# Four of six token-scale rows by two DMAs through DRAM in place of a product with ones, and the gate chain of the forgetting attention one step later

## The chip, the cores and the metric

One core of one Trainium2 chip runs the whole program. The metric is the device time of one execution in microseconds (us); lower is better. TensorE (PE) multiplies, VectorE (DVE) and ScalarE (ACT) work element by element, GpSimd (POOL) does small odd work, and SyncE (SP) issues nearly all DMAs. On a text's engine names, PE, DVE, ACT, POOL and SP are these five.

## What is computed

A trunk of two layers over 512 tokens of 1024 features. Each layer adds half a gated feed-forward network (FFN), a mixer (forgetting attention in the first layer, a sliding-window attention in the second), and half another FFN; a norm stands ahead of each of the six steps and one at the end. Cut to what matters here:

```python
def rms_norm(x, g):
    y = x * lax.rsqrt(jnp.mean(x * x, axis=-1, keepdims=True) + RMS_EPS)
    return y * g

for i in range(2):
    h = h + 0.5 * swiglu(rms_norm(h, norm_g[i, 0]), ffn_w_in[i, 0], ffn_w_out[i, 0])
    h = h + mixer_i(rms_norm(h, norm_g[i, 1]))
    h = h + 0.5 * swiglu(rms_norm(h, norm_g[i, 2]), ffn_w_in[i, 1], ffn_w_out[i, 1])
return rms_norm(h, final_g)

# in the forgetting attention, ahead of the scores:
log_f = log_sigmoid(f_logit + b_f)      # f_logit: 16 of the projected columns
c = cumsum(log_f, axis=time)
```

## The kernel before, in words

**Layout.** The residual `h` lies transposed in SBUF: 128 partitions are features, the free dimension is the 512 tokens, in 8 blocks. A norm is split in two: the gain goes into the activations ahead of the products (`u_hi`, `u_lo`), and the scale of each token, 1/sqrt(mean square), is applied to the result of the products. Every value in a product is split into a high and a low part, so one 128x128 by 128x512 step is three matmuls (`products`, L498).

**Units.** The weights come in 355 units of mostly 128x1024 floats. SP loads a unit into one of four slots of `raw` (L328), ACT rounds it into one of two slots of `w_hi` (L1114), DVE subtracts to get `w_lo` (L1546), PE uses it (24 matmuls for a unit of the FFN input) and counts `unit_used`. ACT takes unit n+2 when unit n has been used. SP may load unit n+4 when `w_lo` of unit n is there (`w_ready`). Each engine's program is written out by hand, so the order of the text is the order on the engine, and semaphores tie them together.

**An FFN** (`ffn`, `in_body`) runs 11 bodies of four units: two units make the gate products in banks 0 and 1, two the up products in banks 2 and 3. DVE multiplies the gate banks with `rstd_row` (L1650), ACT takes silu, DVE multiplies the up banks (L1655) and so on. PE may write the gate banks again, in the next body, when both gate products are scaled (`gate_scaled`). The first body is peeled off, because the token scales are made within it.

**The token scales.** `rstd_row` is the row of 512 scales on all 128 partitions. It is made six times, once for each norm ahead of an FFN or a mixer, numbered nn = 0 to 5:

1. PE sums the squares of each token (`token_sums`, L518) into bank 5, after unit 1 of an FFN body, or after the gate unit of the forgetting attention.
2. DVE makes the mean square `ms` (L1578), POOL raises it to the power -0.5 (`pow_rstd`, L453): `rstd`, 128 partitions by 4, tokens on partitions.
3. DVE scales the identity with each of the four columns (`diagonals`, L1585): `diag`, 128x512.
4. PE multiplies `diag` with a matrix of ones (`row_sums`, L524), so that each partition gets the whole row, in bank 5. In an FFN this stands after unit 2 of the first body.
5. ACT copies it to `rstd_row` (`row_copy`, L1180).

**The forgetting attention** (`fox`) projects V in eight units (k = 0 to 7), with the gate unit (16 columns) after k = 0 and the first query and key units after k = 4. While PE does this, DVE and ACT run the gate chain on 16 partitions: scale and bias, the parts of log-sigmoid (L1765 to L1771 on DVE, Exp and Ln at L1320 and L1323 on ACT), the cumulative sum (L1811 to L1815) and its split (L1327, L1818). V of k = 0 to 3 is scaled out of banks 0 to 3 after k = 3 (ACT L1332, DVE L1825: `v_ready`), and the query unit after k = 4 needs bank 0 of these free.

The lines quoted here say where PE stands in the FFN:

```python
                        mm.then_inc(unit_used, 1)
                        if peeled and r == 1:
                            token_sums(nn, 5)
                        if peeled and r == 2:
                            row_sums(nn)
```

## Time and profile before

| | |
|---|---|
| median of 3 runs | 1869.68 us (1867.63 to 1871.52) |
| the profiled execution | 1868.03 us |
| its span, first to last instruction | 1866.2 us |
| granted TensorE clock over the span | 0.999 |
| PE busy | 1849.2 us, 99% |
| DVE, ACT busy | 926.1 us (50%), 696.1 us (37%) |
| DMA | 181.85 MB, mean 97 GB/s |

How to read it: a group of instructions is named by its line in the kernel, its engine, its operation and the tiles it writes and reads, with how often it ran, its busy time and the mean of one. Matmuls are pipelined: the next one starts before the modelled end of the last, so on PE the distance between two starts tells what one costs, and the duration does not. "Idle before" is the time the engine stood just ahead of an instruction, and the name behind it is what ended that.

### The profile page before, as it was taken

What the parts mean: (1) busy time and instruction counts of PE and PEld (TensorE: products, weight loads), DVE (VectorE), ACT (ScalarE), POOL (GpSimd) and SP (SyncE); (2) the same over time, 40 slices, a digit from 0 to 9 for tenths busy, and PEclk for the clock granted to TensorE, in tenths of its full rate; (3) what the DMA queues carried; (4) which work ended last, traced back from release to release, by engine and by line L of the source; (5) the groups of instructions that cost most, each with busy time, mean ns of one, the idle gap of its engine ahead of it and who ended that gap; (6) DMA issues with size and microseconds to landing.
All of it is one profiled execution on the core that took longest, in us unless ns stands there. A gap on an engine that the chain in (4) does not pass through costs nothing.

```text
span 1866.2 us, 24031 instructions
## 1 busy us (share of the span) xinstructions
PE 1849.2 (99%) x8703; PEld 1522.8 (82%) x8703; DVE 926.1 (50%) x1337; ACT 696.1 (37%) x1149; POOL 24.7 (1%) x44
## 2 busy tenths in 40 slices
PE   9999999999999999999999999999999999999998
PEld 7888888877777888888888888888887888888888
DVE  5444434356887544444334444434379644444332
ACT  5232223245765432323323323323368433232332
POOL 1000000000000000000000000000000000000000
PEclk9999999999999999999999999999999999999999
DMA  4223223323332232222333232223322222222332
GB/s 170 101 91 101 87 89 105 119 95 107 86 94 67 94 102 91 100 97 81 110 107 106 96 101 90 96 88 108 122 79 70 91 93 98 99 92 90 96 104 84
DMA packets 59882, 181.85 MB, mean 97 GB/s; under 512 B 7472, under 2 KB 10032, under 8 KB 59824
## 3 DMA queue, kind: packets, MB, share of 16 engines
q1 hardware_dynamic: 59680, 181.05, 30.0%
q8 instruction: 36, 0.59, 0.1%
...
## 4 chain that ended last, share of the span: by engine, by line
PE 94%; DVE 2%; ACT 2%; issue 1%; DMA 0%; POOL 0%; DVEq 0%; SPq 0%; ACTq 0%; POOLq 0%
PE bank L498 89%; PE bank L874 1%; PE bank L890 1%; ACT scratch L1473 0%; PE bank L906 0%; ACT wide_hi L1423 0%; DVE scratch L2019 0%; PE bank L994 0%; DVE w_lo L1546 0%; PE bank L524 0%; DVE wmax L1969 0%; ACT wide_hi L1279 0%; PE bank L565 0%; DVE wide_lo L1985 0%; DMA scratch<-x_dram 0%
## 5 line engine op out<-in xcount | busy, mean ns | idle before, releaser
L1546 DVE TENSOR_TENSOR w_lo<-raw,w_hi 128x1024 fp32r<-128x1024 f32 (+1 forms) x343 | 392.2, 1143 | 818.5 <-ACT w_hi L1114 817.4
L1114 ACT ACTIVATE w_hi<-raw 128x1024 fp32r<-128x1024 f32 (+1 forms) x343 | 341.1, 995 | 848.1 <-PE bank L498 841.4
L498 PE MATMUL bank<-u_hi,w_hi 128*128 128x512 f32 (+1 forms) x1592 | 630.3, 396 | 0.3 <-DVE w_lo L1546 0.3
L498 PE MATMUL bank<-u_hi,w_lo 128*128 128x512 f32 (+1 forms) x1592 | 620.2, 390 | 0.0
L498 PE MATMUL bank<-u_lo,w_hi 128*128 128x512 f32 (+1 forms) x1592 | 620.2, 390 | 0.0
L498 PEld LDWEIGHTS bank<-u_hi,w_lo 128*128 128x128 f32 (+1 forms) x1592 | 298.1, 187 | 63.9
L498 PEld LDWEIGHTS bank<-u_hi,w_hi 128*128 128x128 f32 (+1 forms) x1592 | 298.6, 188 | 61.0 <-issue 1.1
L498 PEld LDWEIGHTS bank<-u_lo,w_hi 128*128 128x128 f32 (+1 forms) x1592 | 298.5, 188 | 59.1 <-issue 1.0
L498 PE MATMUL bank<-wide_hi,w_hi 128*128 128x512 f32 (+1 forms) x812 | 314.7, 388 | 1.2 <-DVE w_lo L1546 1.1
L498 PE MATMUL bank<-wide_hi,w_lo 128*128 128x512 f32 (+1 forms) x812 | 313.1, 386 | 0.0
L498 PE MATMUL bank<-wide_lo,w_hi 128*128 128x512 f32 (+1 forms) x812 | 313.1, 386 | 0.0
L498 PEld LDWEIGHTS bank<-wide_hi,w_hi 128*128 128x128 f32 x812 | 152.5, 188 | 32.2 <-DVE w_lo L1546 1.3
L498 PEld LDWEIGHTS bank<-wide_hi,w_lo 128*128 128x128 f32 x812 | 152.5, 188 | 30.8
L498 PEld LDWEIGHTS bank<-wide_lo,w_hi 128*128 128x128 f32 x812 | 152.6, 188 | 29.7
L1204 ACT ACTIVATE wide_hi<-scratch 128x512 f32 (+1 forms) x88 | 54.4, 633 | 139.8 <-DVE scratch L1661 139.8
L1665 DVE TENSOR_TENSOR wide_lo<-scratch,wide_hi 128x512 f32 (+1 forms) x88 | 57.0, 689 | 12.9 <-ACT wide_hi L1204 12.5
L1650 DVE TENSOR_TENSOR scratch<-bank,rstd_row 128x512 f32<-128x512 f32 x88 | 56.3, 681 | 1.5 <-PE bank L571 1.5
L1661 DVE TENSOR_TENSOR scratch<-scratch 128x512 f32<-128x512 f32 x88 | 56.4, 682 | 0.0
L1655 DVE TENSOR_TENSOR scratch<-bank,rstd_row 128x512 f32<-128x512 f32 x88 | 56.3, 681 | 0.0
L1198 ACT ACTIVATE scratch<-scratch 128x512 f32<-128x512 f32 x88 | 50.3, 616 | 1.7 <-DVE scratch L1650 1.6
L1360 ACT ACTIVATE wide_hi<-bank 128x512 fp32r<-128x512 f32 (+1 forms) x64 | 28.1, 441 | 41.8 <-PE bank L890 41.6
L1129 ACT ACTIVATE u_hi<-h,gain (+1 forms) x40 | 28.6, 716 | 39.0 <-DVE h L1552 39.0
...
## 6 DMA issues: line engine op xcount, KB each, us to landing
raw<-ffn_in_dram SPq DMA_DIRECT2D x175, 512.0 KB, 3.2
raw<-ffn_out_dram SPq DMA_DIRECT2D x128, 384.0 KB, 3.0
raw<-mix_w_dram SPq DMA_DIRECT2D x51, 512.0 KB, 3.2
wide_hi<-wide_hi SPq DMA_DIRECT2D x28, 128.0 KB, 2.3
y_dram<-raw SPq DMA_DIRECT2D x8, 256.0 KB, 2.7
wide_lo<-wide_lo SPq DMA_DIRECT2D x14, 128.0 KB, 2.3
wide_hi<-wide_hi SPq DMA_DIRECT2D x7, 256.0 KB, 2.8
scratch<-x_dram SPq DMA_DIRECT2D x2, 512.0 KB, 7.1
```

The costliest lines, as they stand in the source:

```text
L498: mm = pe.matmul(out, a, b, start=first and k == 0, stop=last and k == n - 1)
L874: pe.matmul(out, part[:, q_at:q_at + P], part[:, k_at:k_at + nk], start=k == 0 and i > 0, stop=False)
L1114: act.activation(w_hi[:, slot, 0:cols], raw[:, (base + r) % RAW, 0:cols], ACT.Copy)\
L1129: act.activation(dyn(u_hi if nn < 6 else h, m_at), dyn(h, m_at), ACT.Copy, scale=gain[:, bass.ds(8 * nn + i4 + r, 1)]).then_inc(u_hi_ready, 1)
L1198: act.activation(silu_buf[:, c * SEQ:(c + 1) * SEQ], g_scaled_buf[:, c * SEQ:(c + 1) * SEQ], ACT.Silu)\
L1204: act.activation(dyn(wide_hi, 2 * SEQ * i + c * SEQ), up_buf[:, c * SEQ:(c + 1) * SEQ], ACT.Copy)\
L1360: act.activation(wide_hi[:, a:a + cols], bank[5 + at % 2][:, 0:cols], ACT.Copy)\
L1546: dve.tensor_tensor(w_lo[:, s, 0:cols], raw[:, r, 0:cols], f32(w_hi[:, s, 0:cols]), ALU.subtract).then_inc(w_ready, 1)
L1650: dve.tensor_tensor(g_scaled_buf[:, c * SEQ:(c + 1) * SEQ], bank[c][:, :], rstd_row[:, :], ALU.mult).then_inc(gate_scaled, 1)
L1655: dve.tensor_tensor(up_buf[:, c * SEQ:(c + 1) * SEQ], bank[2 + c][:, :], rstd_row[:, :], ALU.mult).then_inc(up_scaled, 1)
L1661: dve.tensor_tensor(up, up, silu_buf[:, c * SEQ:(c + 1) * SEQ], ALU.mult)\
L1665: dve.tensor_tensor(dyn(wide_lo, 2 * SEQ * i + c * SEQ), up_buf[:, c * SEQ:(c + 1) * SEQ], f32(dyn(wide_hi, 2 * SEQ * i + c * SEQ)), ALU.s ...
```

## The change

The row of scales is made by the old way for nn = 0 (first FFN) and nn = 4 (window attention), and by two DMAs for nn = 1, 2, 3 and 5. `ROW_MOVES` and `ROW_PRODUCTS` number these, so that the waits count right. The new way, `place_row` on SP: wait for `rstd`, write its 512 values, 4 bytes each, in token order into a row in DRAM; wait for that DMA; read that row to all 128 partitions of `rstd_row`. For these four norms PE's product, DVE's diagonals and ACT's copy go. SP does this, in an FFN, after the loads of the second body's four units (loads that stood in the loop until now), and in the forgetting attention after the load of its unit 7. In the forgetting attention DVE and ACT do the gate chain one V unit later than before, and PE's wait ahead of k = 4 is for `ms_ready` and the first step of the chain. Waits on `row_ready` become waits on `row_placed`.

```diff
--- before.py
+++ after.py
@@ -44,6 +44,8 @@
 BETWEEN = 4
 FIRST_ORDER = (0, 2, 1, 3)
 FIRST_AT = (11264, 10240)
+ROW_MOVES = {1: 1, 2: 2, 3: 3, 5: 4}
+ROW_PRODUCTS = {0: 1, 4: 2}
 LAST_PAIR = (KB // 2 - 1) * len(OUT_KBS)
 
 
@@ -104,6 +106,7 @@
         sq = sb("sq", [P, 2, SEQ])
         acc = sb("acc", [P, SEQ])
         diag = sb("diag", [P, SEQ])
+        row_dram = nc.dram_tensor("row_dram", (1, SEQ), F32, kind="Internal").ap()
         gain = sb("gain", [P, 7 * KB])
         ident = sb("ident", [P, P])
         ones = sb("ones", [P, P])
@@ -327,7 +332,16 @@
                     sp.wait_ge(w_ready, wait)
                 sp.dma_start(raw[:, slot, 0:cols], src).then_inc(raw_loaded[slot], 16)
 
-            def load_ffn(f):
+            def place_row(nn):
+
+                count = 16 * ROW_MOVES[nn]
+                sp.wait_ge(rstd_ready, nn + 1)
+                sp.dma_start(row_dram.rearrange("o (t p) -> (o p) t", p=P), rstd[:, :], allow_slow_non_contiguous=True)\
+                  .then_inc(row_turned, 16)
+                sp.wait_ge(row_turned, count)
+                sp.dma_start(rstd_row[:, :], row_dram.to_broadcast([P, SEQ])).then_inc(row_placed, 16)
+
+            def load_ffn(f, nn):
                 base = FFN_BASE[f]
 
                 def load_in(i):
@@ -350,7 +364,9 @@
                     load_first()
                 else:
                     load_in(0)
-                with sp.Fori(1, IN_BODIES) as i:
+                    load_in(1)
+                    place_row(nn)
+                with sp.Fori(1 if f == 0 else 2, IN_BODIES) as i:
                     load_in(i)
                 out = base + IN_BODIES * IN_UNITS
                 with sp.Fori(0, (KB // 2) * len(OUT_KBS) // RAW) as i:
@@ -404,13 +420,15 @@
                     if u % 2 and 1 <= j < PAIRS:
                         place_fox_q(j)
                     load((FOX_BASE + u) % RAW, mix_w[u], UNIT, FOX_BASE + u - RAW + 1)
-
-            load_ffn(0)
+                    if u == RAW + 3:
+                        place_row(1)
+
+            load_ffn(0, 0)
             load_fox()
-            load_ffn(1)
-            load_ffn(2)
+            load_ffn(1, 2)
+            load_ffn(2, 3)
             load_window()
-            load_ffn(3)
+            load_ffn(3, 5)
             for t in range(TB):
                 for half_d in range(2):
                     sp.wait_ge((y_scaled_dve, y_scaled_act)[half_d], t + 1)
@@ -520,7 +538,7 @@
                 mm.then_inc(tok_sum, 1)
 
             def row_sums(nn):
-                pe.wait_ge(diag_ready, nn + 1)
+                pe.wait_ge(diag_ready, ROW_PRODUCTS[nn])
                 pe.matmul(bank[5][:, :], ones[:, :], diag[:, :], start=True, stop=True).then_inc(row_sum, 1)
 
             def turn_x(m):
@@ -620,8 +638,6 @@
                         mm.then_inc(unit_used, 1)
                         if peeled and r == 1:
                             token_sums(nn, 5)
-                        if peeled and r == 2:
-                            row_sums(nn)
 
                 if f == 0:
                     first_body()
@@ -832,7 +848,7 @@
                     if k == 0:
                         pe.wait_ge(u_ready, 8 * nn + 2)
                     if k == V_UNITS // 2:
-                        pe.wait_ge(row_ready, nn + 1)
+                        pe.wait_ge(ms_ready, nn + 1)
                         pe.wait_ge(f_chain, 1)
                     for t in range(TB):
                         for q in range(2):
@@ -852,8 +868,6 @@
                         mm.then_inc(unit_used, 1)
                         n += 1
                         token_sums(nn, 5)
-                    if k == 1:
-                        row_sums(nn)
                     if k == V_UNITS // 2:
 
                         for m in range(2):
@@ -1176,7 +1190,7 @@
                 square_x(t)
 
             def row_copy(nn):
-                act.wait_ge(row_sum, nn + 1)
+                act.wait_ge(row_sum, ROW_PRODUCTS[nn])
                 act.activation(rstd_row[:, :], bank[5][:, :], ACT.Copy).then_inc(row_ready, 1)
 
             def ffn(f, nn, last):
@@ -1190,7 +1204,7 @@
                             split_next(r + LOOK - IN_UNITS + 1, base, r, i)
                         else:
                             split_next(base + 4 * i + r + 1, base, r, i)
-                        if type(i) is int and r == 2:
+                        if f == 0 and type(i) is int and r == 2:
                             row_copy(nn)
                         if r == 2:
                             for c in range(2):
@@ -1309,11 +1323,10 @@
                 n += 1
                 step(n)
                 n += 1
-                row_copy(nn)
                 for k in range(1, V_UNITS):
                     step(n)
                     n += 1
-                    if k == 1:
+                    if k == 2:
 
                         act.wait_ge(consts, 1)
                         act.wait_ge(f_chain, 3)
@@ -1322,7 +1335,7 @@
                         act.wait_ge(f_act, 1)
                         act.activation(scratch[0:HEADS, 512:1024], scratch[0:HEADS, 512:1024], ACT.Ln,
                                        bias=ones[0:HEADS, 0:1]).then_inc(f_act, 1)
-                    if k == 2:
+                    if k == 3:
                         act.wait_ge(f_chain, 7)
                         act.activation(decay[0:HEADS, :], scratch[0:HEADS, 0:512], ACT.Copy)\
                            .then_inc(f_act, 1)
@@ -1639,13 +1652,15 @@
                         if first and r == 1:
                             if f == 0:
                                 first_mean_squares()
+                                diagonals(nn)
                             else:
                                 mean_squares(nn, 5)
-                            diagonals(nn)
                         if r == (2 if first else 1):
                             dve.wait_ge(unit_used, base + 4 * i + (3 if f == 0 and first else 2))
-                            if first:
-                                dve.wait_ge(row_ready, nn + 1)
+                            if first and f == 0:
+                                dve.wait_ge(row_ready, ROW_PRODUCTS[nn])
+                            if first and f:
+                                dve.wait_ge(row_placed, 16 * ROW_MOVES[nn])
                             for c in range(2):
                                 dve.tensor_tensor(g_scaled_buf[:, c * SEQ:(c + 1) * SEQ], bank[c][:, :],
                                                   rstd_row[:, :], ALU.mult).then_inc(gate_scaled, 1)
@@ -1759,16 +1774,6 @@
                 mean_squares(nn, 5)
                 step(n)
                 n += 1
-                diagonals(nn)
-                dve.wait_ge(row_ready, nn + 1)
-                dve.wait_ge(unit_used, FOX_BASE + 2)
-                dve.tensor_tensor(x0, bank[4][0:HEADS, :], rstd_row[0:HEADS, :], ALU.mult).then_inc(f_chain, 1)
...
                 def project_scaled(n, is_q, count):
                     if count:
                         dve.wait_ge(qk_ready, count)
@@ -1805,6 +1810,16 @@
                 for k in range(1, V_UNITS):
                     step(n)
                     if k == 1:
+                        dve.wait_ge(row_placed, 16 * ROW_MOVES[nn])
+                        dve.wait_ge(unit_used, FOX_BASE + 2)
+                        dve.tensor_tensor(x0, bank[4][0:HEADS, :], rstd_row[0:HEADS, :], ALU.mult).then_inc(f_chain, 1)
+                        dve.wait_ge(f_chain, 1)
+                        dve.tensor_scalar(x0, x0, bf[:, 0:1], None, ALU.add).then_inc(f_chain, 1)
+                        dve.wait_ge(f_chain, 2)
+                        dve.scalar_tensor_tensor(out=x1, in0=x0, scalar=-1.0, in1=x0, op0=ALU.mult, op1=ALU.max)\
+                           .then_inc(f_chain, 1)
+                        dve.tensor_scalar(x3, x0, 0.0, None, ALU.min).then_inc(f_chain, 1)
+                    if k == 2:
 
                         dve.wait_ge(f_act, 2)
                         dve.wait_ge(f_chain, 4)
@@ -1813,7 +1828,7 @@
                         dve.memset(x3, 1.0).then_inc(f_chain, 1)
                         dve.wait_ge(f_chain, 6)
                         dve.tensor_tensor_scan(x0, x3, x2, 0.0, ALU.mult, ALU.add).then_inc(f_chain, 1)
-                    if k == 2:
+                    if k == 3:
                         dve.wait_ge(f_act, 3)
                         dve.tensor_tensor(decay[32:32 + HEADS, :], x0, f32(decay[0:HEADS, :]), ALU.subtract)\
                            .then_inc(decay_ready, 1)
@@ -1937,7 +1952,7 @@
                 mean_squares(nn, 5)
                 diagonals(nn)
                 dve.wait_ge(biases_ready, 1)
-                dve.wait_ge(row_ready, nn + 1)
+                dve.wait_ge(row_ready, ROW_PRODUCTS[nn])
 
                 def project_scaled(n, j):
                     if j == 1:
```

**Where instructions stand.** On PE, in the first body of the second FFN, before; the `L498` rows ahead of the product are the end of unit 2, those behind it are unit 3:

```order
1789 L498 MATMUL bank<-u_lo,w_hi 128x512
1790 L498 MATMUL bank<-u_hi,w_lo 128x512
1791 L524 MATMUL bank<-diag,ones 128x512 [waits diag_ready]
1792 L498 MATMUL bank<-u_hi,w_hi 128x512 [waits w_ready]
1793 L498 MATMUL bank<-u_lo,w_hi 128x512
```

and with the change, where line 498 has become 516:

```order
1788 L516 MATMUL bank<-u_lo,w_hi 128x512
1789 L516 MATMUL bank<-u_hi,w_lo 128x512
1790 L516 MATMUL bank<-u_hi,w_hi 128x512 [waits w_ready]
1791 L516 MATMUL bank<-u_lo,w_hi 128x512
1792 L516 MATMUL bank<-u_hi,w_lo 128x512
```

The product with ones is gone and nothing stands in its place. On SP, at the start of the second FFN, before:

```order
80 L328 DMA raw<-mix_w_dram 128x1024 [waits w_ready] x4
81 L328 DMA raw<-ffn_in_dram 128x1024 [waits w_ready] x4
82 L353 UNCONDITIONAL_BRANCH
83 L353 ISA
84 L328 ISA [waits w_ready]
85 L328 DMA raw<-ffn_in_dram 128x1024
```

and with the change:

```order
83 L333 DMA raw<-mix_w_dram 128x1024 [waits w_ready] x4
84 L333 DMA raw<-ffn_in_dram 128x1024 [waits w_ready] x8
85 L339 DMA row_dram<-rstd 128x4x1 [waits rstd_ready]
86 L342 DMA rstd_row<-row_dram 128x512 [waits row_turned]
87 L369 UNCONDITIONAL_BRANCH
88 L369 ISA
89 L333 ISA [waits w_ready]
90 L333 DMA raw<-ffn_in_dram 128x1024
```

Eight loads stand ahead of the two new DMAs, the second of which waits for the first; the loop over the other bodies comes behind. On DVE, in the forgetting attention, before:

```order
119 L1546 TENSOR_TENSOR w_lo<-raw,w_hi 128x1024 [waits w_hi_ready]
120 L1585 TENSOR_SCALAR diag<-ident,rstd 128x128 [waits rstd_ready]
121 L1585 TENSOR_SCALAR diag<-ident,rstd 128x128 x3
122 L1765 TENSOR_TENSOR scratch<-bank,rstd_row 16x512 [waits unit_used,row_ready]
123 L1767 TENSOR_SCALAR scratch<-scratch,bf 16x512 [waits f_chain]
124 L1769 SCALAR_TENSOR_TENSOR scratch<-scratch 16x512 [waits f_chain]
125 L1771 TENSOR_SCALAR scratch<-scratch 16x512
126 L1546 TENSOR_TENSOR w_lo<-raw,w_hi 128x1024 [waits w_hi_ready]
127 L1811 TENSOR_TENSOR scratch<-scratch 16x512 [waits f_chain,f_act]
128 L1813 MEMSET scratch 16x512 [waits f_chain]
129 L1815 SCALAR_TENSOR_TENSOR scratch<-scratch 16x512 [waits f_chain]
130 L1546 TENSOR_TENSOR w_lo<-raw,w_hi 128x1024 [waits w_hi_ready]
```

and with the change:

```order
119 L1559 TENSOR_TENSOR w_lo<-raw,w_hi 128x1024 [waits w_hi_ready] x2
120 L1815 TENSOR_TENSOR scratch<-bank,rstd_row 16x512 [waits unit_used,row_placed]
121 L1817 TENSOR_SCALAR scratch<-scratch,bf 16x512 [waits f_chain]
122 L1819 SCALAR_TENSOR_TENSOR scratch<-scratch 16x512 [waits f_chain]
123 L1821 TENSOR_SCALAR scratch<-scratch 16x512
124 L1559 TENSOR_TENSOR w_lo<-raw,w_hi 128x1024 [waits w_hi_ready]
125 L1826 TENSOR_TENSOR scratch<-scratch 16x512 [waits f_chain,f_act]
126 L1828 MEMSET scratch 16x512 [waits f_chain]
127 L1830 SCALAR_TENSOR_TENSOR scratch<-scratch 16x512 [waits f_chain]
128 L1559 TENSOR_TENSOR w_lo<-raw,w_hi 128x1024 [waits w_hi_ready]
129 L1833 TENSOR_TENSOR decay<-scratch,decay 16x512 [waits f_act]
```

One more unit's `w_lo` stands ahead of each part of the chain; the diagonals are gone.

## Rows read from the trace of the kernel before

**Rows 1.** The page's head and part 1: span, and busy time by engine.

```profile
span 1866.2 us, 24031 instructions
...
PE 1849.2 (99%) x8703; PEld 1522.8 (82%) x8703; DVE 926.1 (50%) x1337; ACT 696.1 (37%) x1149; POOL 24.7 (1%) x44
```

**Rows 2.** Waits of PE, largest first: us in total, times, longest us.

```profile
PE bank L498 <- DVE wide_lo L1977: 1.9, 4, 0.6
```

**Rows 3.** Line 524, all six products: min/median/max ns, first and last start us.

```profile
L524 PE MATMUL bank<-diag,ones x12: 592/592/697, 29.8 to 1507.7; 128*128 128x512 f32 x12
```

**Rows 4.** Timeline of PE around the second FFN's product: start us, us, instruction.

```profile
643.69 1.02 PE L524 MATMUL bank<-diag,ones 128*128 128x512 f32 x2
644.15 0.80 PE L498 MATMUL bank<-u_hi,w_hi 128*128 128x512 f32 x1
644.79 0.40 PE L498 MATMUL bank<-u_lo,w_hi 128*128 128x512 f32 x1
...
650.04 0.39 PE L498 MATMUL bank<-u_hi,w_hi 128*128 128x512 f32 x1
```

**Rows 5.** Timeline of DVE in the same body: start us, us, instruction, [idle before].

```profile
638.58 1.23 DVE L1546 TENSOR_TENSOR w_lo<-raw,w_hi 128x1024 fp32r<-128x1024 f32 x1 [4.21 <-ACT w_hi L1114]
639.72 0.15 DVE L1578 TENSOR_SCALAR ms<-bank 128x4 f32<-128x4 f32 x1
...
644.98 1.23 DVE L1546 TENSOR_TENSOR w_lo<-raw,w_hi 128x1024 fp32r<-128x1024 f32 x1 [3.04 <-ACT w_hi L1114]
646.12 1.28 DVE L1650 TENSOR_TENSOR scratch<-bank,rstd_row 128x512 f32<-128x512 f32 x2
```

**Rows 6.** Timeline of POOL in the same body.

```profile
640.02 1.00 POOL L453 TENSOR_TENSOR rstd<-ms,half 128x4 f32<-128x4 f32 x1 [82.97 <-DVE ms L1578]
```

**Rows 7.** DMA issues: count, KB each, median us from issue to landing.

```profile
raw<-ffn_in_dram SPq DMA_DIRECT2D x175, 512.0 KB, 3.2
...
wide_hi<-wide_hi SPq DMA_DIRECT2D x28, 128.0 KB, 2.3
...
wide_hi<-wide_hi SPq DMA_DIRECT2D x7, 256.0 KB, 2.8
...
wide_hi<-wide_lo SPq DMA_DIRECT2D x1, 128.0 KB, 3.7
...
bk<-swa_bk_dram SPq DMA_DIRECT2D x1, 0.5 KB, 6.8
bv<-swa_bv_dram SPq DMA_DIRECT2D x1, 0.5 KB, 6.5
```

**Rows 8.** Timeline of SP's queue at the program's start: issues of two small loads.

```profile
8.41 0.43 SPq L319 DMA_DIRECT2D bk<-swa_bk_dram  x1
8.89 0.43 SPq L320 DMA_DIRECT2D bv<-swa_bv_dram  x1
```

**Rows 9.** Windows in the second FFN; the last two columns are DMA share and GB/s.

```profile
641.90:642.30 0.40, 0.40 (x3) 0.35 (x2) 0.04 (x1) 0.00 (x0) 0.00 (x0) 1.00 0.90 369
642.30:642.70 0.40, 0.40 (x3) 0.33 (x2) 0.00 (x0) 0.00 (x0) 0.00 (x0) 1.00 0.64 256
642.70:643.10 0.40, 0.40 (x4) 0.32 (x3) 0.00 (x0) 0.00 (x0) 0.00 (x0) 1.00 0.08 31
```

**Rows 10.** Timeline in the forgetting attention, POOL, DVE and ACT.

```profile
383.61 2.34 POOL L453 TENSOR_TENSOR rstd<-ms,half 128x4 f32<-128x4 f32 x1 [354.81 <-DVE ms L1578]
...
390.36 0.68 DVE L1765 TENSOR_TENSOR scratch<-bank,rstd_row 16x512 f32<-16x512 f32 x1 [2.71 <-ACT rstd_row L1180]
...
396.33 0.68 DVE L1811 TENSOR_TENSOR scratch<-scratch 16x512 f32<-16x512 f32 x1 [2.60 <-ACT scratch L1323]
...
402.89 1.41 DVE L1825 SCALAR_TENSOR_TENSOR wide_hi<-bank,rstd,wide_hi 128x512 fp32r<-128x512 f32 x2
...
392.34 1.28 ACT L1320 ACT_TABLE_LOAD   x1 [1.07 <-DVE scratch L1769]
...
396.20 1.04 ACT L1114 ACTIVATE w_hi<-raw 128x1024 fp32r<-128x1024 f32 x1
...
398.94 0.63 ACT L1327 ACTIVATE decay<-scratch 16x512 fp32r<-16x512 f32 x1 [1.69 <-DVE scratch L1815]
...
406.09 1.06 ACT L1114 ACTIVATE w_hi<-raw 128x1024 fp32r<-128x1024 f32 x1 [0.77 <-PE bank L498]
```

8 lines of the change are left out of this document (2 added, 6 removed).

## The prediction

> **What bounds the kernel now.** I read the page first: PE is busy for 1849.2 of 1866.2 us [rows 1]. Then the waits of PE: the largest of them is 1.9 us in total [rows 2]. So whatever PE executes is paid for in full, and work of DVE, ACT or DMA costs nothing until PE has to wait for it. Last I read the timelines of the four places that the change touches: on PE for what the removed product costs, on DVE, POOL and the DMA queues for when the row of scales would be there by the new way. The reader should keep two clocks apart: the one of PE, which runs without a gap, and the one of the row, which has a deadline on it.
>
> **Removed from PE.** One product with ones stands in the trace as two matmul records, twelve for the six norms, each with a duration of some 592 ns [rows 3]. The durations overlap, so I take distances between starts. From the first start of the product to the second matmul of unit 3 is 644.79 - 643.69 = 1.10 us [rows 4]. From there to the first matmul of the next body are 23 matmuls in 650.04 - 644.79 = 5.25 us, 0.228 us each. One matmul belongs to the 1.10, so the product costs 1.10 - 0.23 = **0.87 us**. Nothing takes its place: `w_lo` of unit 3, which PE reads next, was done at 638.58 + 1.23 = 639.8, four us before it is asked for [rows 5]. Four products go: 4 x 0.87 = **3.5 us**.
>
> The Trainium skill ("FP8 and Floating Point Precision", section "TensorE Precision Notes") says that true FP32 takes four passes through the array; by that a product would cost 4 x 0.228 = 0.91 us and the four 3.6 us. The trace's 0.87 nearly agrees, and I take the 0.87.
>
> **Removed from DVE and ACT.** The diagonals and the copy: DVE stood idle for 3.04 us ahead of the next `w_lo` in the same body [rows 5], and PE did not wait for either. Worth nothing.
>
> **Added in an FFN: two DMAs in a row, three times.** POOL has `rstd` at 640.02 + 1.00 = 641.02 [rows 6]. The deadline: with the product gone PE starts the second body at 650.04 - 0.87 = 649.17 [rows 4], and it needs both gate banks scaled, which takes DVE 1.28 us [rows 5] and a tenth for the semaphores. The row must be there by 649.17 - 1.38 = **647.8**. It is of no use before 646.12 either, since DVE makes another `w_lo` until then [rows 5]. So there are 6.75 us for both DMAs.
>
> The first DMA (512 pieces of 4 bytes, SBUF to DRAM) is in no row of the trace, so I bound it. It stands behind the load of a weight unit which was issued when `w_lo` was done at 639.8 [rows 5]. That load lands after 3.2 us, at 643.0 [rows 7], and its data flow until 642.7 [rows 9]. The pieces themselves: two small loads of 128 pieces of 4 bytes were issued at 8.41 and 8.89 [rows 8] and landed 6.8 and 6.5 us later [rows 7], at 15.21 and 15.39, one 0.2 us behind the other. Four times as many pieces would take 0.8 us. With 0.4 us from the last data to landing, as for the weight load (642.7 to 643.1), the first DMA lands at 642.7 + 0.8 + 0.4 = 643.9, 2.9 us after its issue. Lower bound: 2.3 us, as the 128 KB moves in SBUF; upper bounds: 3.7 us, the slowest of these that has a row of its own, and far off 6.8 us, the small load at the start behind a full queue [rows 7].
>
> The second DMA (256 KB into SBUF, every partition the same 2 KB) is nearest to the 256 KB moves at 2.8 us; bounds are 2.3 and 3.7 [rows 7]. It starts on an empty queue. The row is there at 641.05 + 2.9 + 0.05 + 2.8 = **646.8**, one us ahead of the deadline. Cost: 0, with a cover of 1.0 us.
>
> Behind SP's wait for the first DMA stands the load of the first unit of the third body. It can't go before `w_lo` of unit 4 is made, at 646.2 [rows 5], when SP has been free since 643.9 + 0.4. It is used four units (22 us) later, so a late SP would cost nothing there. Behind DVE's wait for the row stands the `w_lo` of unit 5, which PE needs 5.5 us after the gate. What is late first is the gate itself. The four loads moved out of the loop keep their place and their waits.
>
> **Added in the forgetting attention: the same two DMAs, and a later chain.** `rstd` is there at 383.61 + 2.34 = 385.95 [rows 10], so the row at 385.95 + 5.8 = 391.75. From DVE's first step of the chain to ACT's Exp are 392.34 - 390.36 = 1.98 us [rows 10]: ACT could begin at 393.7. But now it first rounds unit 5, when PE is done with unit 3. PE finished unit 5 at 406.0 before [rows 10]; a unit is 24 x 0.228 = 5.47 us, so unit 3 ended at 395.1, and with the product gone at 394.2. ACT is free at 394.2 + 1.1 = 395.3, so up to 1.5 us of lateness of the row vanish here. Exp and Ln took 396.20 - 392.34 = 3.9 us: 399.2. DVE's sum took 398.94 - 396.33 = 2.6 us: 401.9. DVE then makes a `w_lo` (1.23), the split of the sum (0.68) and the first V part (0.74): 404.5. PE asks for that part, to get bank 0 back, when unit 5 is done: 406.0 - 0.87 = 405.1. Before, DVE began V at 402.89 [rows 10], and PE had 2.4 us in hand; now 0.6 us are left. Cost: 0 as long as the row is there by 391.75 + 1.5 + 0.6 = 393.9.
>
> **The sum.** -3.5 + 0 + 0 = -3.5 us. The profiled execution took 1868.03 us, which would become 1864.5. It lies 1.65 us below the median of the three runs, inside their spread; against the median 1869.68 the forecast is **1866.2 us**.
>
> **Rivals.**
> *The row is somewhat late.* With both DMAs at 3.7 us the row comes at 641.05 + 3.7 + 0.05 + 3.7 = 648.5, 0.7 after the deadline, three times 2.1 us; in the attention it comes at 393.4 and costs nothing. That gives 1869.7 - 3.5 + 2.1 = 1868.3 us. With half a us more on each DMA it is 1.7 per FFN, 5.1 us, and 0.5 in the attention: 1871.8. For it: two latencies that add up, and a cover of 1.0 us in 5.8. Against it: the usual landing of the nearest rows, 2.3 to 2.8. Chance 0.15.
> *The write of single floats is slow, and the kernel gets slower.* Place: the first DMA, whose landing SP awaits. If it takes x us, an FFN is late by x - 3.9 and the attention by x - 5.05. The kernel is slower by over 0.2% when 3(x - 3.9) + (x - 5.05) passes 3.5 + 3.7 = 7.2, that is from x = 6.0 on. At x = 6.8, the one small load's landing in the trace, the sum is 8.7 + 1.75 - 3.5 = +7.0: 1876.7 us. For it: no row shows 4-byte pieces written to DRAM, each of the 16 engines would get 32 of them if they are spread evenly, and they go to neighbouring addresses. Against it: the 0.2 us for 128 pieces, and that the 6.8 us were spent behind the loads of x and of the first weight units. Chance 0.13.
> The Trainium skill speaks for this rival: "DMA: Bandwidth & Descriptors", section "Rules for kernel authors", says that a non-contiguous last dimension becomes one descriptor per element, and its "Specifications" that below 512 bytes a read-modify-write is done. It gives no price for four bytes, so this changes the chance and not the sum.
> *The products were not on PE's path*, and something else ends their time: 1869.7 us. Against it stands the `w_lo` ready four us early [rows 5]. Chance 0.02.
>
> **Numbers.** 0.2% of the time is 3.7 us, about what a measurement of this kernel can tell from no change. The forecast case has 0.70. Its -3.5 lies just inside that bound, and the three runs spread by 2 us to each side, so it falls on either side of the bound almost evenly: 0.36 faster, 0.34 the same. Of the late row's 0.15, 0.02 are faster, 0.12 the same and 0.01 slower; the slow write is slower with its 0.13; the last is the same with 0.02. Faster 0.38, same 0.48, slower 0.14. The range goes from 3 us below the forecast (the spread of the runs and a median that may itself lie high) to 1870.8, over the greater part of the late row: 0.15 to 0.2 is left out, most of it the slow write.
>
> **What the changed profile would show.** Eight matmul records of the product fewer, and between unit 2 and unit 3 of an FFN's first body the usual distance of 0.23 us. A first DMA that lands 2.9 us and a second that lands 2.8 us after issue. In the FFN's first body, the gate scaling on DVE at 646.2 to 646.8 on the old clock, ahead of PE's second body without a gap. In the attention, Exp right behind ACT's rounding of unit 5, and V scaled 1 us later than before. Wrong would be: a wait of PE's first matmul of the second body for DVE's gate scaling; a wait of the query unit in the attention for V; DVE idle ahead of the gate for a DMA for more than 1.7 us; or a span shorter by less than 3 us without any of these, which would say that PE's 0.87 us were not what the product costs.

## The result and the profile after

| | before | after |
|---|---|---|
| median (lowest to highest), this comparison | 1869.79 us (4 runs) | 1897.61 us (1896.44 to 1900.8, 4 runs) |
| ratio, 95% interval | | 1.0152 [1.0134, 1.017] |
| profiled execution, its span | 1868.03, 1866.2 | 1896.44, 1894.7 |
| granted clock over the span | 0.999 | 0.992 |

The changed kernel is slower by 28 us. The forecast was 1866.2 us with a range up to 1870.8: wrong in sign and far outside the range. The page of the changed kernel, head and part 1, answers to [rows 1]:

```profile
span 1894.7 us, 23961 instructions
...
PE 1855.8 (98%) x8695; PEld 1527.2 (81%) x8695; DVE 922.4 (49%) x1321; ACT 693.7 (37%) x1145; POOL 24.4 (1%) x44
```

The span less PE's busy time is 38.9 us, against 17.0 before: 21.9 us of new idle time. And PE is busy 6.6 us longer, though it executes 3.5 us less. So there are two losses to find. The waits of PE, as in [rows 2]:

```profile
PE bank L516 <- DVE scratch L1665: 18.4, 3, 6.6
PE bank L516 <- DVE w_lo L1559: 4.0, 3, 2.7
PE bank L516 <- DVE wide_lo L1992: 1.9, 4, 0.6
```

Three waits of about 6 us each for the gate scaling, and one of 2.7 us in the forgetting attention. The DMA issues of the changed kernel, the two new kinds, as in [rows 7] (count, KB each, median us to landing):

```profile
rstd_row<-row_dram SPq DMA_DIRECT2D x4, 256.0 KB, 5.0
row_dram<-rstd SPq DMA_DIRECT2D x4, 2.0 KB, 7.9
```

The queue of SP in the second FFN of the changed kernel:

```profile
647.16 0.38 SPq L339 DMA_DIRECT2D row_dram<-rstd  x1
656.07 0.32 SPq L342 DMA_DIRECT2D rstd_row<-row_dram  x1
656.75 8.54 SPq L333 DMA_DIRECT2D raw<-ffn_in_dram  x2
```

SP issues the second DMA when the first has landed: 656.07 - 647.16 = 8.9 us. In the order of the program the four first DMAs take 8.3, 8.9, 7.0 and 7.4 us; the forecast had 2.9. DVE's timeline in the same body of the changed kernel, as in [rows 5]:

```profile
651.08 1.23 DVE L1559 TENSOR_TENSOR w_lo<-raw,w_hi 128x1024 fp32r<-128x1024 f32 x1 [4.56 <-ACT w_hi L1128]
660.63 1.29 DVE L1665 TENSOR_TENSOR scratch<-bank,rstd_row 128x512 f32<-128x512 f32 x2 [8.33 <-DMA rstd_row<-row_dram]
```

PE's timeline there, as in [rows 4]:

```profile
655.00 0.39 PE L516 MATMUL bank<-u_hi,w_lo 128*128 128x512 f32 x1
661.97 0.79 PE L516 MATMUL bank<-u_hi,w_hi 128*128 128x512 f32 x1 [6.59 <-DVE scratch L1665]
...
663.42 0.63 PE L516 MATMUL bank<-u_hi,w_hi 128*128 128x512 f32 x1
663.84 0.63 PE L516 MATMUL bank<-u_lo,w_hi 128*128 128x512 f32 x1
```

DVE waits for the row, and PE for DVE. After the wait PE's matmuls stand 0.42 us apart (663.42 to 663.84), not 0.228. The windows of the same stretch, in the form of [rows 9], say why; the last three columns are granted clock, DMA share, GB/s:

```profile
647.20:649.50 2.30, 2.30 (x12) 1.91 (x11) 0.00 (x0) 0.00 (x0) 0.00 (x0) 1.00 0.64 200
650.00:656.00 6.00, 5.38 (x24) 4.13 (x22) 1.23 (x1) 2.33 (x2) 0.00 (x0) 1.00 0.00 0
656.00:659.50 3.50, 0.00 (x0) 0.00 (x0) 0.00 (x0) 0.00 (x0) 0.00 (x0) 1.00 0.64 59
659.50:662.00 2.50, 0.03 (x1) 0.03 (x1) 1.29 (x2) 0.65 (x2) 0.00 (x0) 0.53 0.65 232
662.00:666.00 4.00, 4.00 (x10) 3.13 (x11) 2.44 (x4) 1.53 (x2) 0.00 (x0) 0.50 0.06 7
666.50:670.00 3.50, 3.50 (x17) 2.88 (x16) 1.98 (x4) 1.29 (x3) 0.00 (x0) 1.00 0.30 116
```

Two things are to be seen. From 650 to 656 the DMA engines show nothing at all, while SP waits for the first DMA. In windows of 0.1 us behind the issues of the four first DMAs, the DMA engines are last busy after 2.4, 2.0, 1.9 and 2.0 us, and from there to the landing pass 5.9, 6.9, 5.1 and 5.4 us. So the pieces are on their way early, and the time goes by between the last activity of the DMA engines and the landing. And the granted clock is 0.50 (1.2 GHz) from about 659.5, after some 4 us in which PE did nothing, until about 666, when it had worked again for 4.4 us.

**The balance.** I went through the granted clock in windows of 4 us over the whole execution: before, it falls only behind the last product at the end of the program; after, it falls five times more, once in each of the three FFNs and twice in the forgetting attention, in the second case at 588, some 190 us after its late row. PE's extra busy time is 6.6 + 3.5 = 10.1 us. By the granted clock PE runs 2.3, 2.5 and 1.7 us short in the three FFNs and twice 1.7 us in the attention, 9.8 us together, which accounts for nearly all of it. The whole is -3.5 (products) + 21.9 (idle) + 10.1 (clock) = +28.5 us. That this is the difference of the spans proves nothing, since a span is PE's busy and idle time together; the evidence is that the new waits (18.4 us in the FFNs, 2.7 + 0.5 in the attention) and the falls fill the two parts.

**By stretch.** As marks I take the starts of POOL's `rstd`, once for each norm (before: [rows 6], [rows 10] and four like them). The change of each stretch against before, in us; "FFN 2, 3, 4" are the stretches that begin with the norm ahead of them:

| kernel | attention | FFN 2 | FFN 3 | window | FFN 4 |
|---|---|---|---|---|---|
| after | +6.03 | +8.09 | +7.43 | -0.19 | +6.98 |
| no row at all | -0.86 | -0.91 | -0.91 | -0.09 | -0.92 |
| DMAs in the attention only | +6.87 | +0.01 | +0.04 | -0.06 | -0.01 |
| the same, `w_lo` ahead of the row | +10.57 | +0.04 | +0.04 | +1.24 | 0.00 |
| two-matmul product | +0.09 | -0.42 | -0.42 | +0.45 | -0.43 |
| 22 filler matmuls | +5.69 | +8.49 | +5.46 | -0.05 | +8.52 |
| 28 filler matmuls | +5.41 | +6.24 | +5.38 | +0.42 | +6.06 |
| 16-byte pieces | +1.98 | -0.40 | -0.60 | +1.19 | +0.13 |
| 16-byte pieces, copied once | -0.94 | -0.71 | -0.25 | +0.22 | -0.05 |

The window stretch moves by up to 1.2 us where nothing in it was changed, so less than that says nothing there.

### The profile page after: what moved, and what is told of

Its sections match the earlier page's. It is cut to its first block, busy times and chain, and to the rows that moved or that the text cites. A ratio compares the mean times of both kernels' runs of the same rounds, so it can differ in the third digit from the quotient of the medians.

```text
span 1894.7 us, 23961 instructions
## 1 busy us (share of the span) xinstructions
PE 1855.8 (98%) x8695; PEld 1527.2 (81%) x8695; DVE 922.4 (49%) x1321; ACT 693.7 (37%) x1145; POOL 24.4 (1%) x44
## 4 chain that ended last, share of the span: by engine, by line
PE 90%; DMA 3%; DVE 3%; ACT 2%; issue 1%; POOL 0%; DVEq 0%; SPq 0%; ACTq 0%; POOLq 0%
PE bank L516 85%; DMA row_dram<-rstd 2%; DMA rstd_row<-row_dram 1%; PE bank L888 1%; PE bank L904 1%; DVE w_lo L1559 1%; PE bank L920 1%; PE bank L1008 0%; ACT scratch L1486 0%; POOL rstd L471 0%; ACT wide_hi L1436 0%; ACT wide_hi L1293 0%; DVE scratch L2034 0%; PE bank L583 0%; DMA scratch<-x_dram 0%
## 5 line engine op out<-in xcount | busy, mean ns | idle before, releaser
L516 PE MATMUL bank<-u_hi,w_hi 128*128 128x512 f32 (+1 forms) x1592 | 632.3, 397 | 19.2 <-DVE scratch L1665 18.4
```

The lines of the kernel that those rows point to most:

```text
L516: mm = pe.matmul(out, a, b, start=first and k == 0, stop=last and k == n - 1)
```

## The experiments

### Was the removed work worth what I took? (norow)

For the four norms neither the product nor the DMAs; `rstd_row` keeps its older content, so this kernel leaves the token scales of four norms out.

```diff
@@ place_row (and the two waits of DVE on row_placed become waits on rstd_ready)
-                sp.dma_start(row_dram.rearrange("o (t p) -> (o p) t", p=P), rstd[:, :], ...)
-                sp.wait_ge(row_turned, count)
-                sp.dma_start(rstd_row[:, :], row_dram.to_broadcast([P, SEQ])).then_inc(row_placed, 16)
+                pass
```

> The changed kernel without its eight new DMAs: for the four norms neither product nor DMA is made, the scales of an earlier norm are used instead (this leaves out part of the computation), and DVE waits for the POOL power alone. Theory A (the removed product is worth 0.87 us of PE each, the later chain and the rest of the change cost nothing, all of the loss comes from waiting for the row): 3.5 us less than before, about 1866 us, PE's total wait as before (largest entry 1.9 us), granted clock 0.999. Rival (part of the loss is in the rest of the change, the shifted chain or the peeled loads): about 1870 us or more, with a new wait of PE in the attention.

Measured: 1865.54 us (11 runs) against 1869.29, ratio 0.998 [0.9971, 0.9989]. Each of the four stretches is shorter by 0.86 to 0.92 us, 3.6 in all. The term of -3.5 us stands, and so does the zero for the later chain, the moved loads and what DVE and ACT no longer do. (Here the chain waits for no row; the last kernel below has the same zero with a row that does come, its attention is shorter by 0.94 us.) All 28 + 3.7 us come from the two DMAs.

### Where does the attention lose? (fox_only, fox_swap)

The first has the DMAs for nn = 1 only. The second also lets DVE make the `w_lo` of unit 5 ahead of its wait for the row.

```diff
@@ both
-ROW_MOVES = {1: 1, 2: 2, 3: 3, 5: 4}
-ROW_PRODUCTS = {0: 1, 4: 2}
+ROW_MOVES = {1: 1}
+ROW_PRODUCTS = {0: 1, 2: 2, 3: 3, 4: 4, 5: 5}
@@ fox_swap, fox on DVE: the first part of the chain behind the next unit's w_lo
-                    if k == 1:
+                    if k == 2:
                         dve.wait_ge(row_placed, 16 * ROW_MOVES[nn])
```

> The DMAs in the forgetting attention only; the three FFNs make their rows by the product again. Theory A (trace of the changed kernel: PE saves 0.9, waits 2.7 + 0.5 us and runs 1.6 us longer at the low clock): 3.9 us more than before, about 1873.7 us, so that 24 of the 28 us lost are the three FFNs'. Rival (the loss is spread over the whole run and belongs to no place): a share of about a quarter, 7 us, about 1877 us.

> As the kernel with DMAs in the attention only, but DVE makes the low part of weight unit 5 ahead of its wait for the row, not behind it. Theory A (PE waits there for the weights queued behind DVE's wait, not for the chain itself): PE's wait for w_lo in the attention falls from 2.7 to 0, no low clock there, the wait for the V part of 0.5 us stays: about 1869.5 us, 4 us less than with the order as it is. Rival (the chain itself is too late): PE waits for the first chain step or V instead, about 1873.7 us as without the swap.

Measured: 1877.26 us, ratio 1.004 [1.0027, 1.0054], and 1877.88 us, ratio 1.0041 [1.0025, 1.0056]. The first lies where the rival had it and 3.6 us above theory A, and still the place is theory A's: the attention's stretch holds the loss, the others move by 0.06 us at most. Theory A's sum had left out the second fall of the clock, at 588. For the second kernel, theory A of the swap is refuted. PE's timeline, only the rows with a wait, with the DMAs in the attention only:

```profile
404.94 0.50 PE L515 MATMUL bank<-w_hi,u_hi 128*128 128x512 f32 x1 [3.39 <-DVE w_lo L1560]
...
412.81 0.47 PE L515 MATMUL bank<-u_hi,w_hi 128*128 128x512 f32 x1 [0.52 <-DVE wide_hi L1839]
```

The same rows of the kernel with `w_lo` ahead of the row:

```profile
401.55 0.47 PE L515 MATMUL bank<-w_hi,u_hi 128*128 128x512 f32 x1 [1.80 <-DVE scratch L1814]
...
412.03 0.77 PE L515 MATMUL bank<-u_hi,w_hi 128*128 128x512 f32 x1 [4.76 <-DVE wide_hi L1838]
```

The swap takes the 3.4 us wait for `w_lo` away, and the time comes back as a wait for V (`wide_hi`), 4.8 us instead of 0.5. In the first kernel PE starts the query unit (the `u_hi` row) 27.35 us behind POOL's `rstd`, in the second 28.37 us behind it, and that 1.0 us is what its two DMAs took longer (8.8 + 5.9 against 7.9 + 5.7). The swap doesn't bring V any earlier. So the `w_lo` queued behind the row was the first to be noticed, and not what set the end: that is the chain from the row over Exp, Ln and the sum to V, as the prediction had followed it. In the first kernel, whose `rstd` is 1.85 us later than before's, the row comes at 401.5 - 1.85 = 399.7 on the old clock, 5.8 us after the predicted deadline of 393.9, and PE starts the query unit at 412.81 - 1.85 = 411.0, 5.9 us after the predicted 405.1. The second kernel's attention is longer by another 3.7 us (+10.57 against +6.87), and that is where the clock falls. Windows of PE (PE busy, granted clock, DMA share, GB/s) around the query unit, with the DMAs in the attention only:

```profile
404.00:408.00 4.00, 3.06 (x10) 0.80 0.40 131
408.00:412.00 4.00, 4.00 (x15) 0.77 0.00 0
```

The same with `w_lo` ahead of the row:

```profile
412.00:416.00 4.00, 3.97 (x9) 0.50 0.25 100
416.00:420.00 4.00, 4.00 (x15) 0.75 0.41 131
```

In the first the fall stands ahead of the query unit, whose start at 412.81 waits for V all the same, by 0.52 us: at full clock PE would only have waited longer, so this fall costs nothing (in this stretch DVE and ACT wait for nothing of PE). In the second it stands behind the longer wait, and PE pays for all of it, 3.0 us.

### What does the fallen clock cost? (warm22, warm28)

Behind the first body of FFN 2, 3 and 4, PE executes 22 or 28 bf16 matmuls of zeros into a bank that nobody reads.

```diff
+                    for _ in range(28):
+                        pe.matmul(bank[7][:, :], warm[:, 0:P], warm[:, :], start=True, stop=True)
```

> The changed kernel with 22 more matmuls of 128x512 bf16 on zeros into a free bank, at the end of the first body of FFNs 2 to 4, where PE stands idle for 5 to 6.6 us (4.7 us of them filled). Theory C (the idle PE drops to the 1.2 GHz level and pays again afterwards): granted clock 1.00 in the 6 us after the wait, 2 to 2.5 us less in each of three FFNs, about 1891 us against 1897.6. Rival (the low clock there has another cause, or costs nothing): 1897 us or more.

> As the kernel with 22 matmuls on zeros, with 28 (6.3 us), so that little of the wait of 5.8 to 7.7 us is left idle. There, with 22, the clock did not fall where 1.3 us were left idle and fell after 2.7 us. Theory C (idle time of about that length lowers the level, and each fall costs 2 us): granted clock 1.00 after all three waits where under 1.5 us are left idle, 2 us less in each, about 1891 to 1893 us. Rival (the fall costs nothing in the end): 1897 us.

Measured: 1896.95 us, ratio 1.0151 [1.0136, 1.0167], and 1893.11 us, ratio 1.0131 [1.0116, 1.0147]. With 22, waits of 2.7, 1.3 and 2.8 us are left in the three FFNs; the clock falls after those of 2.7 and 2.8 us and not after the one of 1.3. Its forecast of 1891 us was missed. Two falls of 1.7 us are left, and from `rstd` to the gate scaling pass 41.8 us in the three FFNs together, against 39.1 in the changed kernel; those 2.7 us more eat up what the third fall gave back. With 28, at most 0.8 us is left and the clock falls in none. The three FFN stretches of the second are 4.8 us shorter than after's, although its rows took 1.1 us longer (40.2 against 39.1 us from `rstd` to the gate scaling): (4.8 + 1.1) / 3 = 2.0 us for each fall, beside a mean of 2.1 from the windows. PE waits for the row either way; the fillers only buy back the clock.

### Could PE pay less for the row without any DMA? (two_parts)

From the kernel before: in FFN 2, 3 and 4 the product is split like all others, into a high and a low part in the rounded type, two matmuls.

```diff
+                if nn in HALVES:
+                    pe.matmul(bank[5][:, :], ones_r[:, :], diag_r[:, :], start=True, stop=False)
+                    pe.matmul(bank[5][:, :], ones_r[:, :], decay[:, :], start=False, stop=True).then_inc(row_sum, 1)
+                    return
```

> The kernel before, with the product of FFNs 2 to 4 made of two reduced-precision (fp32r) matmuls, of a high and a low part of the diagonals, in place of one fp32 product; DVE makes four more small instructions (about 1.2 us) in its idle time. Theory (a matmul of this kind costs PE 0.228 us, the fp32 product 0.87): 0.41 us less at each of three places, 1.2 us in all, about 1868.1 us, too little to be told from no change by the time alone; the distances between starts on PE show it. Rival (DVE's longer diagonals make PE wait): a wait of PE at the product of up to 1 us, no gain or a loss.

Measured: 1868.55 us, ratio 0.9995 [0.9986, 1.0004]. PE's timeline:

```profile
645.06 0.39 PE L529 MATMUL bank<-diag_r,ones_r 128*128 128x512 f32 x1
645.28 0.40 PE L530 MATMUL bank<-decay,ones_r 128*128 128x512 f32 x1
645.52 0.39 PE L502 MATMUL bank<-u_hi,w_hi 128*128 128x512 f32 x1
```

645.52 - 645.06 = 0.46 us instead of 0.87. Each of the three stretches is 0.4 us shorter, and 1.2 us in 1869 can't be told from no change.

### What makes the first DMA slow, and the second? (probe_a, probe_b)

Each kernel tries four forms of both DMAs, one for each norm. They leave out the right scales of three or four norms, or hold them in another order; they are there for their DMAs alone. They write: "plain", as in the change; "sixteen", the row in partition order, 128 pieces of 16 bytes; "whole", one piece of 2 KB; "apart", 512 pieces of 4 bytes, the nearest two 512 bytes from each other (neighbouring partitions 2048). They read back: the row just written, a row of the input, 128 different rows of the input, or 128 rows of SBUF.

```diff
-                sp.dma_start(row_dram.rearrange("o (t p) -> (o p) t", p=P), rstd[:, :], ...)
+                elif write == "sixteen":
+                    to, src = row_dram.rearrange("o (p t) -> (o p) t", t=TB), rstd[:, :]
+                elif write == "apart":
+                    to, src = far_dram[:, :, 0], rstd[:, :]
+                elif write == "whole":
+                    to, src = row_dram, diag[0:1, :]
```

> The changed kernel with another pair of DMAs at each of the four norms (this changes the scales, and so the output). First DMA, SBUF to DRAM: attention 512 pieces of 4 bytes in token order as before; FFN 2: 128 pieces of 16 bytes; FFN 3: one piece of 2 KB from one partition; FFN 4: 512 pieces of 4 bytes, each 512 bytes away from the next. Second DMA, into the row tile: the row just written, 128 times; one row of the input x, 128 times; 128 rows of x; 128 rows out of SBUF. The changed kernel showed 7.0 to 8.9 us from issue to landing of the first and 4.5 to 5.6 of the second. Theory D (the completion of any write to DRAM at this place takes so long): 7 to 9 us for all four first DMAs. Theory P (it is the many small pieces): 2.5 us for the piece of 2 KB, 3 to 5 for the pieces of 16 bytes, 7 to 9 for both kinds of 4 bytes. Theory N (small pieces of several DMA engines that go to the same few hundred bytes wait for each other): 2.5 for the one piece, 3 to 4 for those spread 512 bytes apart, 7 to 9 for those in token order. Second DMA: if 128 reads of one row are slow, one row of x takes 4.5 to 5.6 like the row just written, and 128 rows of x or of SBUF 2.8; if it is the reading of what was just written, one row of x takes 2.8 too.

> As the first probe with the kinds at other places, to part kind and place: attention as before; FFN 2: first DMA one piece of 2 KB, second 128 rows of x; FFN 3: first 512 pieces of 4 bytes 512 bytes apart, second 128 rows out of SBUF; FFN 4: first 128 pieces of 16 bytes, second one row of x 128 times. Every theory: the same times by kind as in the first probe, within a microsecond; a time that stays with the place speaks for the queue's load there.

The queue of SP in the first one; the distance of an L349 to the L360 behind it is the first DMA's time:

```profile
387.04 0.38 SPq L349 DMA_DIRECT2D row_dram<-rstd  x1
395.70 0.33 SPq L360 DMA_DIRECT2D rstd_row<-row_dram  x1
649.57 0.33 SPq L349 DMA_DIRECT2D row_dram<-rstd  x1
652.31 0.33 SPq L360 DMA_DIRECT2D rstd_row<-x_dram  x1
1009.67 0.29 SPq L349 DMA_DIRECT2D row_dram<-diag  x1
1011.78 0.35 SPq L360 DMA_DIRECT2D rstd_row<-x_dram  x1
1511.21 0.60 SPq L349 DMA_DIRECT2D far_dram<-rstd  x1
1514.05 0.50 SPq L360 DMA_DIRECT2D rstd_row<-diag  x1
```

Plain 8.7 us (8.2 in the second kernel), sixteen 2.7 (2.2), whole 2.1 (2.0), apart 2.8 (2.6). The same 512 pieces of 4 bytes take 8.5 us next to each other and 2.7 far apart. So neither a write to DRAM as such is slow, nor the number of pieces. The Trainium skill ("DMA: Bandwidth & Descriptors", "Specifications") says that below 512 bytes a DMA does read-modify-write; the pieces far apart are as small, and only 0.7 us slower than the one of 2 KB. No run here shows whether such a read-modify-write happens. The size alone is not the price here.

The second DMA: the row just written, behind a plain write, 5.7 and 5.6 us; one row of the input to 128 partitions 3.2 to 3.7; 128 different rows 2.7; from SBUF 2.3. So a part of it, 0.5 to 1.0 us, is that all partitions read the same row. The three FFN stretches of each probe are 0.9 us shorter than before's: with any of the fast forms the row is in time.

### How far apart must the pieces be? (probe_c, probe_d)

As above, with 4-byte pieces whose neighbours in the partition direction lie 4 to 64 bytes from each other; they read back a row of the input or the row just written.

```diff
+                    to, src = far_dram[:, 0:P * write].rearrange("t (p s) -> p t s", s=write)[:, :, 0], rstd[:, :]
```

> The changed kernel with first DMAs of 512 pieces of 4 bytes at growing distance between neighbouring partitions (this changes the scales): attention 8 bytes, FFN 2 64 bytes, FFN 3 16 bytes, FFN 4 4 bytes as in the changed kernel. The second DMA is at all four one row of the input x, read 128 times. If pieces that fall into the same 64 bytes wait for each other, the first DMA's time falls with the distance: 7 to 9 us at 4 bytes (16 pieces in 64 bytes), about 5 at 8, about 3.5 at 16, 2.7 at 64. If only pieces of different DMA engines do (eight neighbouring partitions to an engine, so 32 bytes of the row each), it falls at once: 7 to 9 at 4 bytes and 3 from 8 bytes on. If the second DMA is slow because slow writes went ahead, it takes 4.5 us or more at FFN 4 here too; if because the row was just written, 3.2 to 3.7 at all four.

> As the probe before, other kinds at other places: attention 128 pieces of 16 bytes, then the row just written read 128 times; FFN 2 one piece of 2 KB, then the row just written; FFN 3 512 pieces of 4 bytes at a distance of 8 bytes, then the row written two norms ago; FFN 4 pieces of 4 bytes at a distance of 16 bytes, then one row of x. First DMAs as in the other probes by kind. Second DMA: if the reading of a just written row is slow in itself, 4.5 us or more at the attention and FFN 2, 3.2 to 3.7 at FFN 3 and 4; if it was the scattered write behind it, 3.2 to 3.7 at all four.

SP's queue in the first, again issue of the write and of the read behind it:

```profile
387.43 0.38 SPq L349 DMA_DIRECT2D far_dram<-rstd  x1
397.02 0.34 SPq L356 DMA_DIRECT2D rstd_row<-x_dram  x1
648.80 0.38 SPq L349 DMA_DIRECT2D far_dram<-rstd  x1
651.42 0.33 SPq L356 DMA_DIRECT2D rstd_row<-x_dram  x1
1008.90 0.38 SPq L349 DMA_DIRECT2D far_dram<-rstd  x1
1013.35 0.33 SPq L356 DMA_DIRECT2D rstd_row<-x_dram  x1
1511.68 0.38 SPq L349 DMA_DIRECT2D row_dram<-rstd  x1
1520.41 0.34 SPq L356 DMA_DIRECT2D rstd_row<-x_dram  x1
```

| distance of neighbours | probe_c | probe_d |
|---|---|---|
| 4 bytes | 8.7 us | |
| 8 bytes | 9.6 | 8.9 |
| 16 bytes | 4.5 | 4.5 |
| 64 bytes | 2.6 | |
| 128 pieces of 16 bytes, no gap | | 2.5 |
| one piece of 2 KB | | 2.1 |

The time falls from 8 bytes to 16 and from 16 to 64. At 8 bytes it is no shorter than at 4. Both theories forecast a fall there, to 5 us by the pieces in 64 bytes and to 3 us by the DMA engines, so both are refuted as they stand. What the hardware does there stays open; the price by distance is shown.

The row just written is read in 3.8 us behind a write with 16-byte pieces and in 3.0 behind one of 2 KB, so a read of fresh data is not slow as such. Behind plain writes even a row of the input took 5.6 us once, and 3.7 behind the 9.6 us write. Why after's second DMA takes 4.5 to 5.6 us was not settled.

### Pieces of 16 bytes in a kernel with the full computation (rows16, rows16_mix)

`rstd` lies in SBUF with four tokens on each partition, so a row in partition order needs 128 pieces of 16 bytes and no 4-byte ones. Its readers have to step by 16 bytes. In the first kernel all readers of `rstd_row` do:

```diff
-                sp.dma_start(row_dram.rearrange("o (t p) -> (o p) t", p=P), rstd[:, :], ...)
+                sp.dma_start(row_dram.rearrange("o (p t) -> (o p) t", t=TB), rstd[:, :], ...)
@@ and in every reader, here the gate scaling; by_token(t) is t.rearrange("q (p t) -> q t p", t=TB)
-                                dve.tensor_tensor(g_scaled_buf[:, c * SEQ:(c + 1) * SEQ], bank[c][:, :],
-                                                  rstd_row[:, :], ALU.mult).then_inc(gate_scaled, 1)
+                                dve.tensor_tensor(blocks(g_scaled_buf[:, c * SEQ:(c + 1) * SEQ]), blocks(bank[c][:, :]),
+                                                  by_token(rstd_row), ALU.mult).then_inc(gate_scaled, 1)
```

> The changed kernel with the row in DRAM in the order of the partitions: each partition writes its four scales as one piece of 16 bytes (128 pieces, not 512), the row is read to all partitions as it lies, and DVE and ACT go through the tile in token order with a step of 16 bytes. It computes all that the kernel computes. The probes showed 2.2 to 2.7 us for this first DMA, and 3.2 to 3.7 us for reading one row of x 128 times. Theory N2 (the whole loss is the scattered write and what follows from it): the row comes 5.9 to 6.5 us after rstd, within the 6.75 us that an FFN has, PE waits no more than before, and the time is that of the kernel without rows, about 3.6 us less than before: 1865.9 us. Rival 1 (reading a row that was just written takes 4.5 to 5.7 us whatever wrote it): the row comes 0.5 to 1.7 us late in three FFNs, 1867.5 to 1871 us, and the attention loses 0 to 1. Rival 2 (DVE is slower with the step of 16 bytes): its scalings take more than 0.68 us each.

Measured: 1871.34 us (11 runs) against 1869.92, ratio 1.001 [1.0, 1.0019]. With only the order of the row changed, and so 128 pieces of 16 bytes in place of 512 of 4, 26 of the 28 us are back. Its second DMAs take 3.4 to 3.7 us. The kernel's DMA issues, then the gate scaling among the groups of instructions:

```profile
row_dram<-rstd SPq DMA_DIRECT2D x4, 2.0 KB, 2.5
```

The group (count, busy us, mean ns, idle before):

```profile
L1673 DVE TENSOR_TENSOR scratch<-bank,rstd_row 128x512 f32<-128x512 f32 x88 | 88.6, 1048 | 4.6 <-DMA rstd_row<-row_dram 3.1 <-PE bank L597 1.5
```

The first DMA takes 2.4 to 2.8 us instead of 7.0 to 8.9, and from the last activity of the DMA engines to its landing pass 0.4 to 0.9 us. FFN 2 and 3 gain. The scaling reads the row at 1.05 us instead of 0.68, as rival 2 had it, and theory N2's 1865.9 us was missed by 5.4.

The last kernel keeps the step only where there is haste: the second DMA goes to `diag`, the first gate scaling and the chain's first step read that, and ACT copies it once into `rstd_row` for all others.

```diff
+            def row_order(nn):
+                act.wait_ge(row_placed, 16 * ROW_MOVES[nn])
+                act.activation(blocks(rstd_row[:, :]), by_token(diag), ACT.Copy).then_inc(row_ready, 1)
```

> As the kernel with 16-byte pieces, but only the readers that are in a hurry (the gate scaling of the first body of FFN 2, 3 and 4 and the first step of the attention's chain) read the row with a step of 16 bytes; ACT then copies it once into the usual order, and everything later, the window's scalings too, reads that. Theory A: beyond its DMAs the kernel with 16-byte pieces lost its time to the scalings that read with a step (1.05 us instead of 0.68). Then the attention, +2.0 us against the kernel before with all scalings stepped, comes to between -0.9 and 0, the window attention from +1.2 to 0, and the FFNs stay at -0.4, -0.6 and 0, since the row comes at about 647.4 and the two stepped gate scalings end 2.1 us later, some 0.4 us behind the moment at which PE would start its second body. Sum about -1.5 to -2 us: 1868 us, at the edge of what can be told from the kernel before. Theory B: the attention's 2 us came from the row's arrival or from ACT and DVE queueing behind it; then it stays at +1.5 or more (the copy on ACT, 1.1 us behind Ln, adds to it), and the time is 1870 us or more.

Measured: 1867.49 us (1865.58 to 1872.03, 11 runs) against 1869.1, ratio 0.9992 [0.9983, 1.0001]. That is 30 us faster than the change, and not to be told from the kernel before or from the one with the two-matmul product. Its first DMAs take 2.3 to 3.3 us. The stretches are close to theory A: window +0.22, FFNs -0.7, -0.3 and -0.1, attention -0.94. Two groups of DVE, the one with and the one without the step:

```profile
L1691 DVE TENSOR_TENSOR scratch<-bank,rstd_row 128x512 f32<-128x512 f32 x88 | 56.4, 682 | 0.0
...
L1682 DVE TENSOR_TENSOR scratch<-bank,diag 128x512 f32<-128x512 f32 x6 | 6.1, 1071 | 3.8 <-DMA diag<-row_dram 3.8
```

But theory A took too much for the step. Of the attention's 2.9 us between the two kernels a part is the clock: the kernel with all readers stepped has a fall at 584 to 591, the last has none there. Windows of PE in the former (PE busy, granted clock, DMA share, GB/s):

```profile
584.00:588.00 4.00, 3.02 (x10) 0.83 0.37 134
588.00:592.00 4.00, 4.00 (x17) 0.74 0.39 132
```

They are short of full clock by 4 x 0.17 + 4 x 0.26 = 1.7 us. That leaves 1.2 us for the stepped scalings in the attention; and the +1.19 of the window stretch, which I had put on them, is as large as the +1.24 in a kernel without any.

## Why the prediction was wrong, step by step

- **Removed from PE, 0.87 us each.** Right: 0.86 to 0.92 in four stretches without the row, 1865.54 us in all.
- **The deadlines.** Right. In FFN 2 of the changed kernel `rstd` is there at 646.12 + 1.0 = 647.1, so the row was due at 647.1 + 6.8 = 653.9; it came at 660.6, 6.7 us late, and PE waited 6.6. In the attention, with the DMAs there only, a row 5.8 us late brought PE to the query unit 5.9 us late; in the changed kernel both are about 5.1.
- **The first DMA, 2.9 us: the step that failed.** It measured 7.0 to 8.9 us. Its first part was right: I had the last data at 642.7 + 0.8 = 643.5, 2.5 us after the issue, and the DMA engines were last busy 1.9 to 2.4 us after it. The term that failed is the one behind, "With 0.4 us from the last data to landing, as for the weight load": it measured 5.1 to 6.9 us. A weight load, like the small loads that I took the pieces from, writes to 128 different partitions of SBUF; the 512 pieces here go to neighbouring addresses in DRAM, and by the probes just that distance is the price. Why the hardware takes it stays open. All four first DMAs lie above even the far bound of 6.8 us, the landing of `bk`: it was no bound for this mechanism.
- **The second DMA, 2.8 us (bounds 2.3 and 3.7).** Mis-sized too: 4.5 to 5.6 us. With the first at 2.9 us this alone would have brought the row 0.7 to 1.8 us behind the deadline of an FFN. Some 0.5 to 1.0 of it is the common row; the rest stays open.
- **The rival "the write of single floats is slow"** was the right mechanism, at the right place, for one of the reasons named ("they go to neighbouring addresses"). Its formula with the measured x gives (8.9 - 3.9) + (7.0 - 3.9) + (7.4 - 3.9) = 11.6 in the FFNs and 8.3 - 5.05 = 3.3 in the attention; the second DMAs, 1.7 to 2.8 us over the 2.8, add about 9. Sum 24 - 3.5 = +20 us, and what PE paid for late rows, 18.4 us in the FFNs and 5.1 in the attention, less the 3.5, is 20.0. I gave it 0.13 and took x = 6.8 as its end.
- **The clock was left out.** No term and no rival had it: in an FFN a late row costs its lateness and about 2 us again, because the granted clock drops to 1.2 GHz while PE waits. The three falls there cost 6.4 us, a fifth of the way from the forecast to the result. The one behind the late row of the attention costs nothing, since V is later still (PE waits for it another 0.51 us). The one at 588 costs 1.7 us and isn't shown to come from the change. From the forecast on, 18.4 + 5.1 + 6.4 + 1.7 = 31.6 us; the result lies 31.4 above it.
- **"A late SP would cost nothing there"** holds: SP was held up for 9 us, and PE waits for no load in these bodies.
